# A second-block stage of a two-block transformer kernel: gate evacuations from VectorE to ScalarE, two XC operations from VectorE to GpSimd

## The chip, the cores and the metric

The kernel runs on one core of one Trainium2 chip. The metric is the device time of one execution in microseconds; the numbers given are medians over several runs.

## The reference

Two networks run one after the other on 256 tokens of width 1024. The first has two layers (windowed attention, then bidirectional retention, each with a feed-forward part). The second has two equal layers; each has a feed-forward part, a mixer with three branches (windowed attention, a gated linear recurrence, attention over a memory), and a second feed-forward part. The change is in the recurrence branch of the second network's mixer, and in the head norm of the first network's attention. Cut to that:

```python
proj = h @ w_in[l]                       # q, k, v, xr, yr, cq, gates
xc = causal_conv(xr, conv_w) + conv_b    # width 4, per channel
xb = xc.reshape(B, S, LRU_BLOCKS, LRU_BLOCK)
r  = sigmoid(einsum('bshi,hij->bshj', xb, wa) + ba)
gi = sigmoid(einsum('bshi,hij->bshj', xb, wx) + bx)
log_a = -LRU_C * r * softplus(-lam)
a = exp(log_a)
b = sqrt(1 - exp(2 * log_a)) * gi * xc   # the square root is 1 at token 0
h = scan(a, b)                           # h[t] = a[t] h[t-1] + b[t]
br_lru = (h * gelu(yr)) @ w_lru_out
```

The first network's head norm divides each head of q and k by the root of its mean square.

## The kernel before

Every product goes through one pipeline. A weight matrix is cut into units of 512 rows by 256 columns (four chunks of 128 rows). SyncE loads a unit into one of four slots of `raw`; ScalarE rounds it to `w_hi` (line 1234); VectorE computes `w_lo = raw - w_hi` (line 1776); TensorE then makes three matmuls for each chunk and column half, high by high, high by low, low by high (line 845), 24 matmuls of 256 columns a unit, into an accumulator `acc` of two halves used in turn, one half to a block of 256 output columns. A half is given back by the semaphore `acc_free`, which the engine that empties it raises. TensorE starts a unit when `lo_done` says that its `w_lo` is there, and SyncE reloads a slot of `raw` when the split of that slot is done.

ScalarE and VectorE each work through one fixed order of steps, written out by `head`, `step`, `rest` and `evacuate`. For the job that comes next, `head` splits its first three units and after each of them empties what blocks of the job before have ended; `rest` splits the others, with the evacuations three units behind. An engine with nothing to empty for a job passes `None`.

In the second network's layer the jobs around the change are `yr`, `q`, `kvlru`, `gates`, `cq`, `lru_out` and attention. `kvlru` has four units and six blocks. Units 0 and 1 give k and v (blocks 0 and 1, evacuated to `v_T`, which is the tile `std`, and `k_d`). Units 2 and 3 are the block-diagonal gate weights `wa` and `wx`, split into `w_diag`, and give blocks 2 and 3 (`R`) and 4 and 5 (`GI`), 24 matmuls each (line 1176). Before these, TensorE waits for `xc_ok`, the high and low halves of the convolution's result `XC` in `h_hi` and `h_lo`.

- ScalarE casts `XC` to `h_hi` (line 1705, `xch_ok`) after `head("q")`, then goes on with the split of q's last unit. It also takes a sigmoid over all of `R` and all of `GI` (line 1560) once VectorE has written both blocks of each; these sit in ScalarE's order among the splits of `gates` units 1 and 2 and after unit 2.
- VectorE subtracts for `h_lo` after `head("kvlru")` (line 2373), evacuates all six blocks (lines 2095, 2100, 2105: for `R` and `GI` one addition of the bias to 128x1024), and multiplies `GI` by `XC` (`gated_input`, line 2379) after the first iteration of `gates`. The clamp, the multiply by `XR` and the scan follow, each after another iteration of `gates`.
- GpSimd waits for that product (`gx_ok`), then makes attention's biases `bias2` (line 778), and between them the product with `gy` (line 770) and another subtraction for `h_lo` (line 772).

In the first network, the sums of squares of 20 heads stand in rows 0 to 19 of `sd_b`. The matmul of line 1072 spreads them with `headback` over all 128 rows of both, so VectorE first fills `sd_b` with zeros (line 2165).

Of the kernel before, what the change touches and what calls it, by code (L numbers as in the profile page):

```python
# [23 lines left out]
ALU = mybir.AluOpType  # L24
ACT = mybir.ActivationFunctionType

P = 128
D = 1024
DC = D // P
S = 256  # L30
# [257 lines left out]
GATE_B, CONV_W, FFN1_N, MIX_N, CONV_B, BA, BX, LAM, MEM_N, FFN2_N, CUR = 0, 24, 56, 64, 72, 80, 88, 96, 104, 112, 120  # L288
# [20 lines left out]
def build(nc, a, out, const_at):  # L309
    J = JOBS  # L310
    st = ExitStack()
    with st:
# [3 lines left out]
        def sem(name):  # L316
            return st.enter_context(nc.semaphore(name))
# [11 lines left out]
        h_hi, h_lo = h_all[:, 0], h_all[:, 1]  # L329
        rows = sb("rows", [P, 2 * D])  # L330
        prm = sb("prm", [P, 4, P])
        cur = sb("cur", [P, CUR + 16])
# [31 lines left out]
        def arena(*parts):  # L364
# [38 lines left out]
        v_T = std  # L403
# [5 lines left out]
        acc = st.enter_context(nc.psum_tensor("acc", [P, 2, 2, 512], F32))  # L409
        wk = st.enter_context(nc.psum_tensor("wk", [P, 4, 512], F32))  # L410
# [17 lines left out]
        acc_free = sem("acc_free")  # L428
# [15 lines left out]
        hsq, hss, hstd, hrec, hback, hn, hperm, hrot, hqk, kd_ok = [sem(k) for k in (  # L444
            "hsq", "hss", "hstd", "hrec", "hback", "hn", "hperm", "hrot", "hqk", "kd_ok")]
# [9 lines left out]
        cur_ok, conv_ok, xch_ok, xc_ok, zero_ok = [sem(k) for k in ("cur_ok", "conv_ok", "xch_ok", "xc_ok", "zero_ok")]  # L455
        e2_ok, cl_ok, mu_ok, gx_ok, b_ok, scan_ok, lru_ok, lruh_ok, lru_done = [sem(k) for k in (
            "e2_ok", "cl_ok", "mu_ok", "gx_ok", "b_ok", "scan_ok", "lru_ok", "lruh_ok", "lru_done")]
# [3 lines left out]
        yh_ok, y_ok_c, pooled = sem("yh_ok"), sem("y_ok_c"), sem("pooled")  # L461
        ga_ok, gm_ok = sem("ga_ok"), sem("gm_ok")
        low_ok, half_ok, gz_ok, gu_ok, rg_ok = [sem(k) for k in ("low_ok", "half_ok", "gz_ok", "gu_ok", "rg_ok")]
        sd_zero, ri_ok = sem("sd_zero"), sem("ri_ok")
        fin_t, stored = sem("fin_t"), sem("stored")
        fin_ok = [sem("fin_ok_0"), sem("fin_ok_1")]

# [90 lines left out]
        HEAD_ORDER = [8, 9] + list(range(8))  # L558
# [142 lines left out]
        def _(pool):  # L701
# [59 lines left out]
            for l in range(LAYERS2):  # L761
                pooled_squares("dna", l)

                pool.wait_ge(gx_ok, 1 + l)
                first, _, _ = attn_base("second", l)
                for h in range(WH):
                    if h == 2:

                        pool.wait_ge(scan_ok, 8 + l * 8)
                        pool.tensor_tensor(XC[:], XR[:, :, 0:S], gy[:], ALU.mult).then_inc(lru_ok, 1)  # L770
                        pool.wait_ge(lruh_ok, 1 + l)
                        pool.tensor_tensor(h_lo[:, :, S:2 * S], XC[:], h_hi[:, :, S:2 * S], ALU.subtract).then_inc(lru_done, 1)
                    if h >= 4:

                        pool.wait_ge(m_raw, first + 4 * ((h - 4) // 2) + 4)
                    pool.wait_ge(in_const, 16 * 2)

                    pool.tensor_tensor(bias2[:, h % 4, :], alibi[:, :], slopes[:, h:h + 1].broadcast_to((P, 2 * S)), ALU.mult)\
                        .then_inc(bias_ok, 1)

                for b in range(J["mem_out"].per):
                    pool.wait_ge(mgh_ok, 1 + b + l * 4)
                    pool.tensor_tensor(h_lo[:, 2 * b:2 * b + 2, S:2 * S], gates[:, 2 * b:2 * b + 2, :], h_hi[:, 2 * b:2 * b + 2, S:2 * S],
                                       ALU.subtract).then_inc(mg_done, 1)
                pooled_squares("w_out", l)
                pooled_squares("dnb", l)
# [3 lines left out]
        def _(pe):  # L790
# [277 lines left out]
            for c in range(11):  # L1068
                if c < 10:
                    if c >= 2:  # L1070
                        pe.wait_ge(hn, c - 1)
                    pe.matmul(wk[:, 1 + c % 2, :], headback[:, HEAD_ORDER[c], :], sd_b[:, 0, :], start=True, stop=True).then_inc(hback, 1)
                if c:
                    b = c - 1
                    pe.wait_ge(hn, b + 1)
                    if b >= 2:
                        pe.wait_ge(hrot, b - 1)
                    pe.matmul(part_ps[b % 2][:, 0:S], partner[:, :], qk[:, HEAD_ORDER[b], 0:S], start=True, stop=True).then_inc(hperm, 1)
                beside_first(c - 11)
# [63 lines left out]
            for l in range(LAYERS2):  # L1143
# [14 lines left out]
                for p in range(2):  # L1158
                    unit_ready(job, l, 0, p)
                    for cb in range(2):  # L1160
                        for k in range(KCH):
                            for i, (ws, xs) in enumerate(((w_hi, h_hi), (w_hi, h_lo), (w_lo, h_hi))):
                                mm = pe.matmul(acc[:, 1 - cb, 0, 0:S], ws[:, p, k, cb * P:(cb + 1) * P], xs[:, p * KCH + k, 0:S],
                                               start=(p == 0 and k == 0 and i == 0), stop=(p == 1 and k == KCH - 1 and i == 2))
# [63 lines left out]
        def _(act):  # L1228
# [325 lines left out]
                ins.then_inc(acc_free, 1)  # L1554

            def kvlru(l, it, b):
                if b in (3, 5):
                    dst = R if b == 3 else GI
                    act.wait_ge(acc_free, J["kvlru"].taken(l, 0, b))
                    act.activation(dst[:], dst[:], ACT.Sigmoid).then_inc(ri_ok, 1)  # L1560

            def q_e(l, it, b):
                act.copy(q_2[:, 2 * b:2 * b + 2, :], acc[:, b, :, 0:S]).then_inc(acc_free, 1)
# [31 lines left out]
                    act.wait_ge(hss, c - 1)  # L1595
                act.activation(sq_b[:, c % 2, :], qk[:, c, :], ACT.Square).then_inc(hsq, 1)
            act.wait_ge(hss, 10)
            act.wait_ge(sd_zero, 1)
            act.activation(sd_b[0:20, 0, :], wk[0:20, 0, :], ACT.Sqrt, bias=eps[0:20, 0:1], scale=1.0 / HD).then_inc(hstd, 1)
            act.preload_act_table(ACT.Exp)  # L1600
            for i in range(-SIDE_START - 1, 0):
# [169 lines left out]
        def _(dve):  # L1771
# [34 lines left out]
            def head(name, l=None, prev=None, prev_evac=None):  # L1806

                for p in range(LAG):
                    step(name, l, 0, p)
                    if prev:  # L1810
                        evacuate(prev, prev_evac, prev_layer(prev, name, l), J[prev].iters - 1, J[prev].body + p - LAG)
                if isinstance(prev_evac, tuple):
                    prev_evac[1](prev_layer(prev, name, l), J[prev].iters - 1)

            def rest(name, evac, l=None, between=(), first=LAG):


                job, late = J[name], evac[1] if isinstance(evac, tuple) else None
                for p in range(first, job.body):
                    step(name, l, 0, p)  # L1820
                    evacuate(name, evac, l, 0, p - LAG)

                def one(it):
                    for p in range(job.body):
                        step(name, l, it, p)
                        if p < LAG:
                            evacuate(name, evac, l, it - 1, job.body + p - LAG)
                        else:
                            evacuate(name, evac, l, it, p - LAG)
                        if late and p == LAG:  # L1830
                            late(l, it - 1)

                for n, other in enumerate(between):
                    if n:
                        one(n)
                    other()
                start = max(len(between), 1)
                if job.iters > start:
                    with dve.Fori(start, job.iters) as it:
                        one(it)  # L1840
# [249 lines left out]
                        dve.tensor_tensor(bb(0), bb(0), bb(2), ALU.add).then_inc(mg_ok, 1)  # L2090
                return evac

            def kvlru(l, it, b):
                if b == 0:
                    dve.tensor_copy(v_T[:], acc[:, 0, 0, 0:S]).then_inc(acc_free, 1)
                elif b == 1:

                    for g in range(2):
                        for half in range(2):
                            ins = dve.tensor_copy(k_d[64 * half:64 * half + 64, g, :], acc[64 * g:64 * g + 64, 1, 0, 0:S])  # L2100
                    ins.then_inc(acc_free, 1)
                else:
                    dst, bias = (R, BA) if b < 4 else (GI, BX)
                    c = 4 * (b % 2)
                    dve.tensor_tensor(dst[:, c:c + 4, :], acc[:, b % 2].rearrange("p a (c t) -> p (a c) t", c=2),  # L2105
                                      cur[:, bias + c:bias + c + 4].unsqueeze(2).broadcast_to((P, 4, S)), ALU.add).then_inc(acc_free, 1)

            def modulations(n, layer, src, c0, c1):

                dve.tensor_tensor(mod[:, layer, c0:c1, :], src, prm[:, 0, 48 * layer + c0:48 * layer + c1].unsqueeze(2)  # L2110
# [51 lines left out]
            dve.wait_ge(in_prm, 16 * PRM_DMAS)  # L2162
            dve.wait_ge(soft_ok, 1)
            dve.scalar_tensor_tensor(soft_t[:], soft_in[:], -1.0, soft_in[:], ALU.mult, ALU.min).then_inc(soft_v, 1)
            dve.memset(sd_b[:, 0, :], 0.0).then_inc(sd_zero, 1)
            dve.wait_ge(in_attn, 96)
            dve.wait_ge(hstd, 1)
            dve.reciprocal(sd_b[0:20, 0, :], sd_b[0:20, 0, :]).then_inc(hrec, 1)
# [1 line left out]
            for c in range(11):  # L2170
# [6 lines left out]
                if c:  # L2177
                    b = c - 1
# [139 lines left out]
            for l in range(LAYERS2):  # L2318
# [50 lines left out]
                conv(3)  # L2369
                rest("q", None, l)  # L2370
                head("kvlru", l, "q", None)
                dve.wait_ge(xch_ok, 1 + l)
                dve.tensor_tensor(h_lo[:, :, S:2 * S], XC[:], h_hi[:, :, S:2 * S], ALU.subtract).then_inc(xc_ok, 1)
                rest("kvlru", kvlru, l)
                head("gates", l, "kvlru", kvlru)

                def gated_input():
                    dve.wait_ge(ri_ok, 2 + l * 2)
                    dve.tensor_tensor(GI[:], GI[:], XC[:], ALU.mult).then_inc(gx_ok, 1)

                def clamp():
                    dve.wait_ge(e2_ok, 8 + l * 16)
# [12 lines left out]
                    for c in range(DC):  # L2395
                        dve.tensor_tensor_scan(XR[:, c, 0:S], R[:, c, :], GI[:, c, :], 0.0, ALU.mult, ALU.add).then_inc(scan_ok, 1)

                rest("gates", None, l, [gated_input, clamp, multiply, scan])
                head("cq", l, "gates", None)
                dve.wait_ge(vt_ok, 1 + l)  # L2400
                dve.tensor_copy(v_2[:].rearrange("p r n -> p (r n)"), wk[:, 3, 0:S]).then_inc(v2_ok, 1)
# [66 lines left out]
```

## Time and profile before

| | us |
|---|---|
| median of 3 runs | 2594.54 |
| lowest and highest run | 2586.8, 2594.69 |
| the profiled execution | 2586.8 |
| its span, from the first to the last instruction | 2585.0 |
| TensorE busy (share of the span) | 2485.5 (96%) |
| VectorE busy | 1535.9 (59%) |
| ScalarE busy | 1254.2 (49%) |
| GpSimd busy | 113.3 (4%) |

The profile is of one execution. PE is TensorE, DVE VectorE, ACT ScalarE, POOL GpSimd and SP SyncE. Times in its rows are counted from the start of the span. Layer 0 of the stage in question lies at 1513 to 1550 us, layer 1 at 2176 to 2213.

### The profile page before, as it was taken

The numbers are of one execution on the slowest core, as the hardware profiler recorded it, in microseconds if no ns is written. First come the engines' busy times: TensorE is split into PE (matmuls) and PEld (weight loads), VectorE is DVE, ScalarE is ACT, GpSimd is POOL, SyncE is SP. The second block draws the span as 40 slices with busy tenths as digits, with TensorE's granted clock in tenths as the row PEclk, the third lists the DMA queues.
The fourth block names the chain that finished last, engine by engine and source line by source line (L and its number), as shares of the span: only waits on it lengthen the run. The fifth ranks groups of instructions, "written<-read, shape, count | busy, mean of one in ns | idle before, by whom it ended". The sixth has DMA issues, their size and how long they took to land.

```text
span 2585.0 us, 42115 instructions
## 1 busy us (share of the span) xinstructions
PE 2485.5 (96%) x15422; PEld 2131.8 (82%) x15422; DVE 1535.9 (59%) x2452; ACT 1254.2 (49%) x1911; POOL 113.3 (4%) x104
## 2 busy tenths in 40 slices
PE   7999989999989999999999999999999999999998
PEld 5745678888879976788888989898888899989887
DVE  4166553332264256666776666877667766676874
ACT  3257532222243252554555458655555544865553
POOL 3000000000000000000000001110000000111000
PEclk9999999999999999999999999999999999999999
DMA  8389323333232242465565545356556555444653
GB/s 277 96 269 293 116 74 96 93 96 97 90 114 90 89 136 95 145 194 180 180 186 168 181 146 187 106 173 191 184 180 191 162 174 181 157 133 147 195 181 119
DMA packets 398653, 398.25 MB, mean 154 GB/s; under 512 B 17360, under 2 KB 396768, under 8 KB 398544
## 3 DMA queue, kind: packets, MB, share of 16 engines
q1 hardware_dynamic: 395680, 390.25, 48.3%
q0 software_dynamic: 2864, 6.57, 0.8%
q8 instruction: 66, 1.08, 0.2%
q14 instruction: 43, 0.35, 0.0%
HBM read 395.72 MB, written 1.05 MB: 153 GB/s over the span
## 4 chain that ended last, share of the span: by engine, by line
PE 81%; DVE 6%; issue 5%; ACT 4%; POOL 2%; DMA 1%; SPq 0%; ACTq 0%; DVEq 0%; POOLq 0%
PE acc L845 28%; PE acc L839 25%; PE acc L841 13%; PE acc L824 4%; DVE w_lo L1776 2%; ACT w_hi L1234 2%; PE acc L908 1%; PE wk L975 1%; PE wk L1002 1%; PE acc L1002 1%; PE wk L927 1%; PE acc L1203 1%; PE wk L917 1%; POOL XC L770 1%; PE wk L988 1%
## 5 line engine op out<-in xcount | busy, mean ns | idle before, releaser
L1776 DVE TENSOR_TENSOR w_lo<-raw,w_hi 128x1024 fp32r<-128x1024 f32 (+1 forms) x656 | 803.9, 1239 | 601.4 <-ACT w_hi L1234 600.2
L1234 ACT CAST w_hi<-raw 128x1024 fp32r<-128x1024 f32 (+1 forms) x656 | 669.3, 1032 | 458.1 <-PE acc L845 231.2
L845 PE MATMUL acc<-h_all,w_hi 128*128 128x256 f32 (+1 forms) x3360 | 750.6, 319 | 22.6 <-DVE GI L2105 6.9
L839 PE MATMUL acc<-h_all,w_hi 128*128 128x512 f32 x2016 | 710.5, 397 | 4.5 <-DVE h_all L1885 4.5
L845 PEld LDWEIGHTS acc<-h_all,w_hi 128*128 128x128 f32 x3360 | 563.3, 193 | 67.5 <-issue 20.8
L841 PE MATMUL acc<-h_all,w_lo 128*128 128x256 f32 x2016 | 565.5, 281 | 0.0
L845 PE MATMUL acc<-h_all,w_lo 128*128 128x256 f32 (+1 forms) x1680 | 534.9, 318 | 0.0
L839 PEld LDWEIGHTS acc<-h_all,w_hi 128*128 128x128 f32 x2016 | 379.7, 188 | 94.3 <-issue 4.7
L841 PEld LDWEIGHTS acc<-h_all,w_lo 128*128 128x128 f32 x2016 | 382.2, 190 | 0.2
L845 PEld LDWEIGHTS acc<-h_all,w_lo 128*128 128x128 f32 x1680 | 323.8, 193 | 20.7
L839 PE MATMUL acc<-hid_all,w_hi 128*128 128x512 f32 x880 | 312.4, 398 | 2.9 <-DVE w_lo L1776 2.9
L841 PE MATMUL acc<-hid_all,w_lo 128*128 128x256 f32 x880 | 247.6, 281 | 0.0
L839 PEld LDWEIGHTS acc<-hid_all,w_hi 128*128 128x128 f32 x880 | 165.2, 188 | 45.4 <-DVE w_lo L1776 4.8
L841 PEld LDWEIGHTS acc<-hid_all,w_lo 128*128 128x128 f32 x880 | 165.9, 189 | 0.1
L824 PE MATMUL acc<-w_hi,h_all 128*128 128x256 f32 x704 | 128.1, 284 | 0.0
L2027 DVE TENSOR_TENSOR act_buf<-acc,act_buf 128x512 f32<-128x512 f32 x110 | 76.0, 691 | 84.0 <-ACT act_buf L1500 54.4
L824 PEld LDWEIGHTS acc<-w_hi,h_all 128*128 128x128 f32 x704 | 110.1, 192 | 1.8 <-issue 1.7
L845 PE MATMUL acc<-hid_all,w_hi 128*128 128x512 f32 x352 | 111.0, 396 | 0.0
L824 PE MATMUL acc<-w_lo,h_all 128*128 128x256 f32 x352 | 99.6, 283 | 0.0
L845 PEld LDWEIGHTS acc<-hid_all,w_hi 128*128 128x128 f32 x352 | 66.1, 188 | 15.9
L1500 ACT COPY act_buf<-acc 128x512 f32<-128x512 f32 x55 | 32.3, 587 | 94.4 <-PE acc L841 94.4
L1397 ACT ACTIVATE probs<-probs,soft_nm 128x256 f32<-128x256 f32 (+1 forms) x112 | 63.2, 564 | 26.9 <-DVE soft_nm L1925 26.1
(346 smaller groups left out, 2446.8 us busy)
## 6 DMA issues: line engine op xcount, KB each, us to landing
raw<-in_w_in_dram SPq DMA_DIRECT2D x100, 512.0 KB, 3.9
ring<-in_ada_w_dram SPq DMA_DIRECT2D x88, 512.0 KB, 5.6
raw<-in_ffn_w_in_dram SPq DMA_DIRECT2D x88, 512.0 KB, 3.6
raw<-in_ffn_w_gate_dram SPq DMA_DIRECT2D x88, 512.0 KB, 3.9
raw<-in_ffn_w_up_dram SPq DMA_DIRECT2D x88, 512.0 KB, 3.9
raw<-in_ffn_w_down_dram SPq DMA_DIRECT2D x80, 512.0 KB, 4.3
raw<-in_ret_w_qkvg_dram SPq DMA_DIRECT2D x48, 512.0 KB, 3.7
raw<-in_ffn_w_out_dram SPq DMA_DIRECT2D x40, 512.0 KB, 3.5
```

Of the source, the lines that this page charges most:

```text
L770: pool.tensor_tensor(XC[:], XR[:, :, 0:S], gy[:], ALU.mult).then_inc(lru_ok, 1)
L824: mm = pe.matmul(o, xs[:, kk, x], ws[:, s, k, :], start=(u == 0 and k == 0 and i == 0 and not (packed and n % 2)), stop=(last and k == nk ...
L839: pe.matmul(o, w_hi[:, s, k, c], merged[:, :, kk, t], start=(u == 0 and k == 0), stop=False, skip_group_check=True)
L841: mm = pe.matmul(o[:, S:2 * S], w_lo[:, s, k, c], merged[:, 0, kk, t], start=False, stop=(last and k == nk - 1), skip_group_check=True)
L845: mm = pe.matmul(o, ws[:, s, k, c], xs[:, kk, t], start=(u == 0 and k == 0 and i == 0), stop=(last and k == nk - 1 and i == 2))
L908: mm = pe.matmul(acc[32 * k:32 * k + 32, b % 2, 0, 0:S], c_wide[:, u * KCH + k, :], landed[:, k, :], start=(u == 0), stop=(u == 1), tile_p ...
L1002: mm = pe.matmul(G["out"], G["v"][c], G["probs_t"][:, 2 * (q % 2) + n, c, :], start=(c == 0), stop=(c == tiles - 1), skip_group_check=True)
L1234: act.copy(w_hi[:, s, 0:nk, :], raw[:, s, 0:nk, :]).then_inc(hi_done, 1)
L1397: act.activation(pr, pr, ACT.Exp, bias=snm[:, i % 8:i % 8 + 1], accum_out=ssum[:, i % 8:i % 8 + 1])\
L1500: act.copy(up, acc[:, 1, :, S:2 * S]).then_inc(low_ok, 1)
L1776: dve.tensor_tensor(w_lo[:, s, 0:nk, :], raw[:, s, 0:nk, :], w_hi[:, s, 0:nk, :], ALU.subtract).then_inc(lo_done, 1)
L2027: dve.tensor_tensor(part, acc[:, b, :, 0:S], part, ALU.add).then_inc(acc_free, 1)
```

## The change

Five things are edited.

1. ScalarE empties all six blocks of `kvlru`: two of them with plain copies, the four gate blocks with sigmoids of 128x256 straight out of the accumulator, the bias in the same instruction, four a block. The two sigmoids of 128x2048 and the semaphore `ri_ok` go, and VectorE's `kvlru` evacuation goes.
2. The subtraction for `h_lo` of `XC` is done by GpSimd, when `xch_ok` is there.
3. The product of `GI` and `XC` is done by GpSimd, when `acc_free` says that the last block of `kvlru` is out, and ahead of the biases.
4. In VectorE's order `gated_input` becomes an empty entry.
5. The matmul of line 1072 reads 20 rows of `headback` and `sd_b`; the memset and its semaphore `sd_zero` go.

```diff
@@ GpSimd
-                pool.wait_ge(gx_ok, 1 + l)
+                pool.wait_ge(xch_ok, 1 + l)
+                pool.tensor_tensor(h_lo[:, :, S:2 * S], XC[:], h_hi[:, :, S:2 * S], ALU.subtract).then_inc(xc_ok, 1)
+
+                pool.wait_ge(acc_free, J["kvlru"].done(l))
+                pool.tensor_tensor(GI[:], GI[:], XC[:], ALU.mult).then_inc(gx_ok, 1)
@@ TensorE
-                    pe.matmul(wk[:, 1 + c % 2, :], headback[:, HEAD_ORDER[c], :], sd_b[:, 0, :], start=True, stop=True).then_inc(hback, 1)
+                    pe.matmul(wk[:, 1 + c % 2, :], headback[0:20, HEAD_ORDER[c], :], sd_b[0:20, 0, :], start=True, stop=True).then_inc(hback, 1)
@@ ScalarE
             def kvlru(l, it, b):
-                if b in (3, 5):
-                    dst = R if b == 3 else GI
-                    act.wait_ge(acc_free, J["kvlru"].taken(l, 0, b))
-                    act.activation(dst[:], dst[:], ACT.Sigmoid).then_inc(ri_ok, 1)
+                if b == 0:
+                    act.copy(v_T[:], acc[:, 0, 0, 0:S]).then_inc(acc_free, 1)
+                elif b == 1:
+
+                    for g in range(2):
+                        for half in range(2):
+                            ins = act.copy(k_d[64 * half:64 * half + 64, g, :], acc[64 * g:64 * g + 64, 1, 0, 0:S])
+                    ins.then_inc(acc_free, 1)
+                else:
+                    dst, bias = (R, BA) if b < 4 else (GI, BX)
+                    for c in range(4):
+                        cc = 4 * (b % 2) + c
+                        ins = act.activation(dst[:, cc, :], acc[:, b % 2, c // 2, (c % 2) * S:(c % 2) * S + S], ACT.Sigmoid,
+                                             bias=cur[:, bias + cc:bias + cc + 1])
+                    ins.then_inc(acc_free, 1)
...
-            act.wait_ge(sd_zero, 1)
@@ VectorE
-            def kvlru(l, it, b):
-                if b == 0:
-                    dve.tensor_copy(v_T[:], acc[:, 0, 0, 0:S]).then_inc(acc_free, 1)
-                elif b == 1:
...
-            dve.memset(sd_b[:, 0, :], 0.0).then_inc(sd_zero, 1)
...
-                dve.wait_ge(xch_ok, 1 + l)
-                dve.tensor_tensor(h_lo[:, :, S:2 * S], XC[:], h_hi[:, :, S:2 * S], ALU.subtract).then_inc(xc_ok, 1)
-                rest("kvlru", kvlru, l)
-                head("gates", l, "kvlru", kvlru)
-
-                def gated_input():
-                    dve.wait_ge(ri_ok, 2 + l * 2)
-                    dve.tensor_tensor(GI[:], GI[:], XC[:], ALU.mult).then_inc(gx_ok, 1)
+                rest("kvlru", None, l)
+                head("gates", l, "kvlru", None)
...
-                rest("gates", None, l, [gated_input, clamp, multiply, scan])
+                rest("gates", None, l, [lambda: None, clamp, multiply, scan])
```

## Rows read from the trace of the kernel before

**Rows 1.** The page's chain that ended last, shares by engine.

```profile
PE 81%; DVE 6%; issue 5%; ACT 4%; POOL 2%; DMA 1%; SPq 0%; ACTq 0%; DVEq 0%; POOLq 0%
```

**Rows 2.** TensorE's waits, 1513 to 1550 us: total, times, longest.

```profile
PE acc L845 <- DVE GI L2105: 3.4, 1, 3.4
PE acc L1176 <- DVE R L2105: 1.4, 1, 1.4
PE acc L1163 <- ACT rows L1563: 0.7, 1, 0.7
PE acc L1176 <- DVE std L2095: 0.6, 1, 0.6
```

**Rows 3.** Timeline of ScalarE in the stage: start, duration, instruction, idle before.

```profile
1513.52 1.90 ACT L1705 CAST h_all<-XC 128x2048 fp32r<-128x2048 f32 x1 [0.78 <-DVE XC L2360]
1515.32 1.99 ACT L1234 CAST w_hi<-raw 128x1024 fp32r<-128x1024 f32 x2
...
1535.35 1.92 ACT L1560 ACTIVATE R<-R 128x2048 f32<-128x2048 f32 x1 [5.17 <-DVE R L2105]
1537.18 1.02 ACT L1234 CAST w_hi<-raw 128x1024 fp32r<-128x1024 f32 x1
...
1543.76 1.28 ACT L1281 ACT_TABLE_LOAD   x1
```

**Rows 4.** Timeline of VectorE in the stage.

```profile
1516.40 3.62 DVE L1776 TENSOR_TENSOR w_lo<-raw,w_hi 128x1024 fp32r<-128x1024 f32 x3 [2.91 <-ACT w_hi L1234]
...
1529.06 0.42 DVE L2095 COPY std<-acc 128x256 f32<-128x256 f32 x1 [0.52 <-PE acc L1163]
...
1532.88 2.36 DVE L2105 TENSOR_TENSOR R<-acc,cur 128x1024 f32<-128x1024 f32 x2 [0.51 <-PE acc L1176]
...
1539.37 2.35 DVE L2105 TENSOR_TENSOR GI<-acc,cur 128x1024 f32<-128x1024 f32 x2
```

**Rows 5.** Timeline of TensorE in the stage.

```profile
1522.04 0.28 PE L845 MATMUL acc<-h_all,w_lo 128*128 128x256 f32 x1
...
1534.25 3.04 PE L1176 MATMUL acc<-h_all,w_diag 128*128 128x256 f32 x24 [1.41 <-DVE R L2105]
1540.72 0.75 PE L845 MATMUL acc<-h_all,w_hi 128*128 128x256 f32 x2 [3.43 <-DVE GI L2105]
...
1544.05 0.47 PE L845 MATMUL acc<-h_all,w_hi 128*128 128x256 f32 x2
```

**Rows 6.** Stretches: width, busy time of PE, PEld, DVE, ACT, POOL, granted clock, DMA.

```profile
1540.70:1544.40 3.70, 3.68 (x18) 3.68 (x19) 1.02 (x1) 2.54 (x2) 0.00 (x0) 0.54 0.46 140
1550.00:1560.00 10.00, 10.00 (x84) 9.85 (x83) 5.95 (x5) 9.94 (x16) 1.68 (x2) 1.00 0.47 134
```

**Rows 7.** GpSimd on tile XC: ns min/median/max, first and last start.

```profile
L770 POOL TENSOR_TENSOR XC<-XR,gy x2: 7783/7785/7787, 1586.1 to 2248.6; 128x2048 f32<-128x2048 f32 x2
...
L772 POOL TENSOR_TENSOR h_all<-XC,h_all x2: 4634/4634/4634, 1614.5 to 2277.1; 128x2048 fp32r<-128x2048 f32 x2
```

**Rows 8.** VectorE's line 1776, 1590 to 1597 us and 1612 to 1626 us.

```profile
L1776 DVE TENSOR_TENSOR w_lo<-raw,w_hi x2: 1211/2704/4197, 1590.7 to 1594.8; 128x1024 fp32r<-128x1024 f32 x2
...
L1776 DVE TENSOR_TENSOR w_lo<-raw,w_hi x4: 1212/2055/4814, 1615.4 to 1624.1; 128x1024 fp32r<-128x1024 f32 x4
```

**Rows 9.** ScalarE's line 1553 (gates evacuations): durations, and two of them in the timeline.

```profile
L1553 ACT ACTIVATE gates<-acc,cur x48: 465/474/486, 1553.0 to 2274.8; 128x256 f32<-128x256 f32 x24, 128x256 f32 x24
...
1552.98 0.84 ACT L1553 ACTIVATE gates<-acc,cur 128x256 f32<-128x256 f32 x2
```

**Rows 10.** TensorE at 97.42 us in the timeline, and the stretch after it.

```profile
97.42 0.70 PE L845 MATMUL acc<-h_all,w_hi 128*128 128x512 f32 x2 [1.83 <-DVE w_lo L1776]
...
97.40:102.00 4.60, 4.58 (x20) 3.81 (x21) 4.03 (x6) 2.25 (x3) 0.00 (x0) 1.00 0.75 226
```

**Rows 11.** The page's loads of the input projection: KB each, us to landing.

```profile
raw<-in_w_in_dram SPq DMA_DIRECT2D x100, 512.0 KB, 3.9
```

**Rows 12.** TensorE's first head-norm matmuls in the timeline.

```profile
134.08 3.40 PE L1072 MATMUL wk<-sd_b,headback 128*128 128x512 f32 x4 [4.21 <-DVE sd_b L2168]
```

More of the change, by code:

```diff
@@ L463, in build @@
         low_ok, half_ok, gz_ok, gu_ok, rg_ok = [sem(k) for k in ("low_ok", "half_ok", "gz_ok", "gu_ok", "rg_ok")]
-        sd_zero, ri_ok = sem("sd_zero"), sem("ri_ok")
         fin_t, stored = sem("fin_t"), sem("stored")
@@ L2091, in branch @@
                 return evac
-            def kvlru(l, it, b):
-                if b == 0:
-                    dve.tensor_copy(v_T[:], acc[:, 0, 0, 0:S]).then_inc(acc_free, 1)
-                elif b == 1:
[L2098 to L2106, printed above, removed]
             def modulations(n, layer, src, c0, c1):
```

## The prediction

> **What bounds the kernel now.** I read the page's chain first: TensorE holds most of it [rows 1], so one microsecond taken from or given to TensorE is one microsecond of the span, and work on the other engines counts only where TensorE waits for it. Then, for the stretch of the change (kvlru, once in each layer of the second block), TensorE's waits: four of them, 3.4, 1.4, 0.7 and 0.6 us [rows 2]. Layer 1 repeats layer 0 662.6 us later (2277.1 - 1614.5 [rows 7]), so I work in layer 0 and double. The 0.7 us wait is for a q copy that the change leaves alone; the other three, 5.4 us a layer, are for the evacuations that it moves. The timelines of ScalarE and VectorE say why the longest is so long. The last gate matmuls start at 1534.25 and end 3.04 us later, at 1537.29 [rows 5], but VectorE takes the accumulator only at 1539.37 [rows 4]. In its queue stands the split of gates unit 2, which waits for ScalarE's cast at 1537.18, and that cast stands behind the sigmoid of R at 1535.35, which waited for VectorE's own evacuation of R [rows 3, 4]. TensorE starts again at 1540.72, and at half clock: granted 0.54 over the next 3.7 us, with 18 matmuls [rows 6]. The pace at full clock is (3.04 - 0.28) / 23 = 0.12 us a matmul [rows 5]; at the low level (1.2 GHz instead of 2.4) it is 3.33 / 16 = 0.21. The sixteen slow matmuls from 1540.72 to 1544.05 [rows 5] cost 3.33 - 16 x 0.12 = 1.4 us more. So at most 5.4 + 1.4 = 6.8 us a layer are to be had, 13.6 in all, 0.5% of the span.
>
> **The parts of the change.** The sum is made against the profiled execution, 2586.8 us (span 2585.0). It is the lowest of the three runs; the median is 2594.54, 7.7 us above it, and I carry the difference over to the median.
>
> (1) The subtraction for the low half of XC goes from VectorE to GpSimd and starts as soon as ScalarE's cast is done: 1513.52 + 1.90 = 1515.42 [rows 3], with GpSimd idle. The same form, fp32r out of two 128x2048 inputs in SBUF, took 4.63 us on GpSimd [rows 7]. It would run from 1515.46 to 1520.09. Its consumers, the gate matmuls, start behind the v_T copy of 1529.06 [rows 4], so as a result it is early by 9 us. But look at what VectorE's splits did while GpSimd ran such an operation [rows 7, 8]. A split takes 1.21 us. The one begun at 1590.7, under the multiply that ended at 1586.1 + 7.8 = 1593.9, took 4.20 and ended 1.0 us after it. The first of four begun from 1615.4 on, under the subtraction that ended at 1614.5 + 4.6 = 1619.1, is the longest, 4.81, and ended 1.1 us after it. A two-input fp32 operation of VectorE stands still until GpSimd's is over. In the new place the split of q's last unit stands there: its w_hi is cast just behind XC's cast, and it ran from 1516.40 [rows 3, 4]. Now it ends at 1520.09 + 1.09 = 1521.18. TensorE wants it at the start of that unit's 24 matmuls: 1522.04 - 23 x 0.12 = 1519.28 [rows 5]. New wait: **+1.9 us**. The kvlru splits behind it (1.2 us each) are ready before TensorE gets to them, and the loads that wait for these splits to free their slots, 3.9 us to landing [rows 11], are wanted some 6 us later.
>
> The Trainium skill says the same of the pair (SBUF - State Buffer, section SBUF: two separate sides): the SBUF ports that VectorE and GpSimd share are an exclusive lock, held for a whole instruction, and the loser blocks. By that rule the trace agrees [rows 8], and the rule speaks against the change. The Trainium skill's page GPSIMD Engine Reference (section Elementwise - side-by-side cycle accounting) puts this size at 4497 ns where the row has 4634; by the page the new wait would be 1.8 instead of 1.9 us.
>
> (2) Blocks 0 and 1 (v_T and k_d) are copied by ScalarE at the same trigger. A 128x256 ScalarE operation out of PSUM takes 0.47 us [rows 9], VectorE's copy 0.42 [rows 4]; TensorE's wait is the 0.6 us before the gate matmuls [rows 2]. Between 0 and 0.1 either way: **0**. The cast of gates unit 1, now behind these five copies, is wanted 10 us later.
>
> (3) Blocks 2 and 3 (R): VectorE took one 128x1024 operation a block, 2.36 for two [rows 4]. ScalarE takes four sigmoids a block, at a pace of 0.84 - 0.47 = 0.37, the first block after 3 x 0.37 + 0.47 = 1.58 us; 0.84 is what two of this kind take in the gates stretch, and 0.47 is one [rows 9]. TensorE's wait was 1.41 with about 1.2 of evacuation in it [rows 2, 5], and becomes 1.41 + 0.36: **+0.35 us**. The second half's accumulator is free at 8 x 0.37, as the twelve matmuls before it end. From below this could be 0.2 (four at 0.31 after a shorter first), from above 0.6.
>
> (4) Blocks 4 and 5 (GI): nothing stands before them on ScalarE now but one cast of 1.02 us [rows 3], which is over while the matmuls run (3.04). The wait becomes 1.58 + 0.15 = 1.73 us where it was 3.43 [rows 5]: **-1.7 us**. The big sigmoids (1.92 for R [rows 3], and one like it for GI) vanish: ScalarE's next work, the table load at 1543.76, starts when block 5 is done, which is 1537.29 + 1.9 + 0.35 + 3.08 = 1542.6, 1.1 us earlier. That matters, for ScalarE is busy 9.94 of 10 us in the gates stretch [rows 6], so it has little room there; but its start moves up by more than TensorE's, and it does not hold TensorE back through this change.
>
> (5) The clock. TensorE starts gates at 1540.72 + 1.9 + 0.35 - 1.7 = 1541.3, after a pause of 1.7. A pause of 1.83 us left the granted clock at 1.00 [rows 10]; the fall came after 3.43 [rows 5, 6]. So I take it that the slow matmuls go: **-1.4 us**.
>
> (6) GI times XC goes to GpSimd: 1542.6 to 1547.3 at 4.63. VectorE's split of gates unit 3 is cast at about 1545 and ends at 1548.4; TensorE wants it at 1541.3 + 3 x 2.88 = 1549.9. The product is wanted by VectorE's multiply two iterations of gates later, the two biases behind it only by attention. **0**. What VectorE loses in work nobody waits for beyond what is counted above.
>
> (7) The head sums: one memset of VectorE, issued long before ScalarE writes over it, and a contraction over 20 rows instead of 128, in 20 matmul instructions paced by their 512 columns; TensorE's 4.2 us wait, up to 134.08, is for a reciprocal that stays [rows 12]. **0**, within half a microsecond.
>
> Sum for a layer: 1.9 + 0.35 - 1.7 - 1.4 = -0.85 us, two layers **-1.7 us**: 2585.1 for the profiled execution, 2592.8 for the median.
>
> **The rivals.** Within 0.3% (7.8 us) is about what a measurement of this kernel cannot tell from no change.
> (a) The forecast: the new wait for GpSimd eats what the shorter evacuation gives; only the clock is won. 0.6.
> (b) The clock falls all the same, since the stretch now holds pauses of 1.9, 0.6, 1.8 and 1.7 us. Then +0.55 a layer, 2595.6. Against it only the single pause of [rows 10]. 0.13.
> (c) GpSimd's subtraction does not stand in the split's way, as that is finished by both in turns. Then no 1.9: -2.75 a layer, -5.5, 2589.0. Against it both rows of [rows 8]. 0.09.
> (d) The other side: GpSimd takes for such an operation what the multiply of 128x2048 took, 7.79 [rows 7]. I think that part of those was its own waiting for a VectorE operation that was already running, but it may be the price of the operation. Then the split ends 3.15 us later, the pause becomes 5.1 and the clock falls (+1.4), and the product in (6) ends so late that gates unit 3 is 1.6 us late: -0.85 + 3.15 + 1.4 + 1.6 = +5.3 a layer, +10.6, 2605.1. It makes the kernel slower by over 0.3% from about 7.1 us an operation. 0.06.
> (e) The move of the evacuations does nothing, since ScalarE comes to block 4 no earlier than VectorE did (a late load holds the cast of gates unit 2). Then 1.7 + 1.4 of the gain goes, -0.85 becomes +2.25 a layer, +4.5, 2599.0. Against it: loads land in 3.9 us [rows 11], and the slot is free as soon as VectorE has split the gate weights, some 10 us before the cast. 0.06.
> Something elsewhere that I don't see: 0.06, half to each side.
>
> **The numbers.** Predicted is (a), 2592.8. The runs of one kernel spread by 7.9 us here, more than any of (a) to (c) moves it, so the range reaches from 2584 (the profiled execution's level less the forecast) to 2600, with (b), (c) and (e) in it; outside stand (d) and most of the unseen. Faster by over 0.3%: 0.07, from the unseen (0.03) and from a (c) that comes with shorter evacuations, or falls on the low side of the spread (0.04). Slower by over 0.3%: 0.09, (d) with 0.06 and the unseen with 0.03. Same: 0.84.
>
> **What would show it.** After the change, the split of q's last unit should last over 4 us, and TensorE should have a wait for it of 1.9 us near 1521; the wait at the first R evacuation should be 1.7 to 1.8 and that before gates 1.7, with the clock at 1.00 behind it. GpSimd's subtraction should take 4.6 and its product 4.6. The prediction is wrong if the product or the split holds TensorE a second time, if the clock falls, or if q's last split is not stretched.

## The result and the profile after

The kernel got slower. After the change the median is 2606.32 us (5 runs, 2603.89 to 2608.22), before it 2592.01 us (5 runs beside them, 2586.8 to 2594.69): a ratio of 1.0055, 95% interval 1.004 to 1.0069. The forecast was 2592.8, added up from the three-run median of 2594.54, with a range up to 2600. The profiled execution of the changed kernel took 2607.67 us, with a span of 2605.9.

Most of the difference lies in one slice of the page. These are its rows of TensorE's granted clock in 40 slices of 65 us, of the kernel before and then of the kernel after:

```profile
PEclk9999999999999999999999999999999999999999
```

```profile
PEclk9979999999999999999999999999999999999999
```

The third slice, 130 to 195 us, holds the head norm of the first network, the place of the change's fifth edit. Its loop reaches from the first matmul that spreads the head sums to the first attention score. First the stretches of the kernel before: width, busy time of PE, PEld, DVE, ACT, POOL with instruction counts, granted clock, DMA share, GB/s; the first row is the whole loop, the others its beginning.

```profile
134.08:156.30 22.22, 21.32 (x113) 9.01 (x113) 18.22 (x40) 6.32 (x12) 0.00 (x0) 0.92 0.60 188
134.00:139.00 5.00, 4.92 (x9) 2.37 (x10) 2.24 (x5) 0.00 (x0) 0.00 (x0) 0.66 0.25 79
139.00:144.00 5.00, 5.00 (x36) 2.16 (x35) 4.91 (x12) 2.02 (x4) 0.00 (x0) 1.00 0.26 78
```

The same of the kernel after:

```profile
135.27:172.86 37.59, 37.28 (x113) 11.41 (x113) 19.24 (x40) 6.31 (x12) 0.00 (x0) 0.55 0.38 117
135.00:140.00 5.00, 4.73 (x6) 1.65 (x6) 1.71 (x3) 0.00 (x0) 0.00 (x0) 0.50 0.30 95
140.00:145.00 5.00, 5.00 (x7) 1.50 (x6) 3.12 (x7) 0.00 (x0) 0.00 (x0) 0.50 0.00 0
150.00:155.00 5.00, 5.00 (x23) 1.46 (x22) 3.32 (x8) 2.37 (x5) 0.00 (x0) 0.69 0.80 252
155.00:160.00 5.00, 5.00 (x14) 1.38 (x14) 2.00 (x5) 1.68 (x3) 0.00 (x0) 0.50 0.47 142
175.00:180.00 5.00, 4.60 (x52) 1.90 (x45) 4.04 (x21) 4.13 (x14) 0.00 (x0) 1.00 0.95 302
```

The same 113 matmuls take 37.59 us instead of 22.22, which is 15.4 us more, and TensorE is busy for 37.28 of them: it waits for nobody. Busy time times clock is nearly the same, 21.32 x 0.92 = 19.6 before and 37.28 x 0.55 = 20.5 after. So TensorE does the same work at a lower clock: 0.50 is the 1.2 GHz level, 1.00 the 2.4 GHz level. Before, the clock falls to the low level in the loop's first microsecond, behind a pause of 4.2 us [rows 12], and is at 1.00 again from 138 us on. After, it comes up near 149 us, falls again at 152 us with no gap in TensorE's work, and is back at 1.00 for good only when the attention that follows is running. By the distances between starts, the twenty edited matmuls take 7.2 us of the 15.4 more, the 93 others 8.2.

Single calls in the timeline of the kernel after show both levels:

```profile
135.27 3.77 PE L1075 MATMUL wk<-sd_b,headback 20*128 20x512 f32 x4 [4.21 <-DVE sd_b L2165]
...
150.64 1.12 PE L1075 MATMUL wk<-sd_b,headback 20*128 20x512 f32 x2
...
157.82 2.07 PE L1075 MATMUL wk<-sd_b,headback 20*128 20x512 f32 x2
```

and one of the kernel before, at 1.00:

```profile
143.85 1.13 PE L1072 MATMUL wk<-sd_b,headback 128*128 128x512 f32 x2
```

At equal clock a call over 20 rows takes what one over 128 rows takes, 1.12 and 1.13 us (x2: each call is recorded as two matmuls). The pause ahead of the first call is as before, 4.21 us.

The stage that the prediction worked on came out as forecast in this execution. TensorE's waits there after the change, 1536 to 1570 us (total, times, longest), answer to [rows 2]:

```profile
PE acc L848 <- DVE w_lo L1789: 1.8, 1, 1.8
PE acc L1179 <- ACT R L1572: 1.8, 1, 1.8
PE acc L848 <- ACT GI L1572: 1.7, 1, 1.7
PE acc L1166 <- ACT rows L1577: 0.7, 1, 0.7
PE acc L1179 <- ACT std L1561: 0.6, 1, 0.6
```

VectorE's three splits beside the new place of the subtraction, with the group of that line in 1536 to 1545 us (min/median/max ns) behind them, and GpSimd's two new operations (the last two rows):

```profile
1537.17 7.06 DVE L1789 TENSOR_TENSOR w_lo<-raw,w_hi 128x1024 fp32r<-128x1024 f32 x3 [2.91 <-ACT w_hi L1237]
```

```profile
L1789 DVE TENSOR_TENSOR w_lo<-raw,w_hi x3: 1211/1212/4794, 1537.2 to 1543.0; 128x1024 fp32r<-128x1024 f32 x3
```

```profile
L764 POOL TENSOR_TENSOR h_all<-XC,h_all x2: 4610/4613/4616, 1536.3 to 2197.9; 128x2048 fp32r<-128x2048 f32 x2
L767 POOL TENSOR_TENSOR GI<-GI,XC x2: 4627/4627/4627, 1563.4 to 2225.0; 128x2048 f32<-128x2048 f32 x2
```

The first split begins 0.9 us after GpSimd's subtraction and takes 4.79 us where 1.21 is its length; it ends at 1537.17 + 4.79 = 1541.96, and TensorE, which has waited 1.8 us for it, starts at 1542.02. The matmuls that start gates, and the stretch behind them, answer to [rows 5, 6]:

```profile
1561.97 0.50 PE L848 MATMUL acc<-h_all,w_hi 128*128 128x256 f32 x2 [1.74 <-ACT GI L1572]
```

```profile
1561.90:1565.60 3.70, 3.63 (x30) 3.64 (x31) 0.00 (x0) 3.67 (x6) 2.22 (x1) 1.00 0.47 142
```

The clock is 1.00 there, where it was 0.54. From the start of ScalarE's cast of XC to the same matmul at the end of gates' second unit, layer 0 takes 1567.70 - 1534.29 = 33.41 us, where it took 1547.95 - 1513.52 = 34.43: 1.0 us less, and 0.9 less in layer 1.

So 15.4 us more in the head norm and 1.9 less in the two layers make 13.5, where the medians differ by 14.3. The two profiled executions differ by more, 2607.67 - 2586.8 = 20.9 us. The remaining 7.4 us lie in stretches in which the kernels are the same: 1.2 us ahead of the loop, 4.2 between the loop and the first cast of XC, the rest behind it. Read in steps of 4 us, TensorE's clock stands at the low level for about 44 us of the 1361 between loop and cast in the changed kernel's trace, for about 34 of 1357 before. Work takes twice as long there, so by an estimate from these numbers the 10 us account for up to 5. Low stretches of this kind also stand in the trace of the kernel before, one of them with TensorE busy all the time:

```profile
172.00:175.00 3.00, 3.00 (x16) 1.49 (x14) 0.00 (x0) 0.69 (x3) 0.00 (x0) 0.51 1.10 350
```

Why one execution has more of them than another is not explained here.

### The profile page after: what moved, and what is told of

The parts are those of the page before. It is cut to its first block, busy times and chain, and to the rows that moved or that the text cites. A ratio compares the mean times of both kernels' runs of the same rounds, so it can differ in the third digit from the quotient of the medians.

```text
span 2605.9 us, 42125 instructions
## 1 busy us (share of the span) xinstructions
PE 2504.9 (96%) x15422; PEld 2133.5 (82%) x15422; DVE 1525.9 (59%) x2429; ACT 1262.1 (48%) x1949; POOL 133.7 (5%) x108
## 3 DMA queue, kind: packets, MB, share of 16 engines
HBM read 395.72 MB, written 1.05 MB: 152 GB/s over the span
## 4 chain that ended last, share of the span: by engine, by line
PE 81%; DVE 7%; ACT 5%; issue 5%; POOL 2%; DMA 1%; SPq 0%; ACTq 0%; DVEq 0%; POOLq 0%
PE acc L848 27%; PE acc L842 25%; PE acc L844 12%; PE acc L827 4%; DVE w_lo L1789 2%; ACT w_hi L1237 2%; PE acc L911 1%; PE wk L978 1%; PE wk L1005 1%; PE acc L1005 1%; PE wk L1075 1%; PE wk L930 1%; PE acc L1206 1%; PE wk L920 1%; POOL XC L773 1%
## 5 line engine op out<-in xcount | busy, mean ns | idle before, releaser
L1789 DVE TENSOR_TENSOR w_lo<-raw,w_hi 128x1024 fp32r<-128x1024 f32 (+1 forms) x656 | 815.3, 1257 | 614.0 <-ACT w_hi L1237 612.8
```

The costliest lines, as they stand in the source:

```text
L1789: dve.tensor_tensor(w_lo[:, s, 0:nk, :], raw[:, s, 0:nk, :], w_hi[:, s, 0:nk, :], ALU.subtract).then_inc(lo_done, 1)
```

## The experiments

Each kernel below was run beside the kernel before on the same chip, and its ratio is against those runs. The theories are named in the expectations themselves.

### The head norm alone, undone and done

Undone: the changed kernel with 128 rows and the zeros back (in the diffs of this section `...` stands for the rest of a line, and the waits for `sd_zero` are not shown).

```diff
+            dve.memset(sd_b[:, 0, :], 0.0).then_inc(sd_zero, 1)
-                    pe.matmul(wk[:, 1 + c % 2, :], headback[0:20, HEAD_ORDER[c], :], sd_b[0:20, 0, :], ...)
+                    pe.matmul(wk[:, 1 + c % 2, :], headback[:, HEAD_ORDER[c], :], sd_b[:, 0, :], ...)
```

> The changed kernel with the matmul of line 1072 back at 128 rows, and the memset with it. Theory H: the 20-row contraction costs the 15.4 us by which the changed trace is longer between its first matmul of that line and the third block of attention scores (135.27 to 177.91 against 134.08 to 161.35), as TensorE's granted clock stands at 0.50 to 0.69 there. Then this kernel takes the time before less the 2 us of the kvlru stage, 2590 (ratio 0.998 to 1.000). Rival L: the loss lies in the rest of the program (the two traces drift apart by another 7.5 us there). Then this kernel stays some 5 to 7 us slower than before, ratio 1.002 to 1.003.

Done alone: the kernel before with 20 rows and without the memset, and nothing else of the change.

> The kernel before with the 20-row matmul alone, memset gone. Theory H: plus 15 us, ratio 1.006, the clock at 0.5 to 0.7 in the head norm. Rival L: within 0.3% of before. Rival M, that the loss comes from both parts together: less than half of it here.

Undone, the time is 2588.91 us (12 runs), a ratio of 0.9987, interval 0.9978 to 0.9997. Alone, it is 2604.89 us (6 runs), 1.005, interval 1.0034 to 1.0067. Theory H came out, L and M are out. The loop in each, as a stretch; undone first:

```profile
135.57:157.83 22.26, 21.31 (x113) 8.92 (x113) 18.18 (x40) 6.32 (x12) 0.00 (x0) 0.93 0.59 188
```

```profile
132.95:170.53 37.58, 37.22 (x113) 11.41 (x113) 19.24 (x40) 6.32 (x12) 0.00 (x0) 0.55 0.38 118
```

The loop is 22.3 us at 0.93 with 128 rows and 37.6 us at 0.55 with 20, whatever is done in the second network. The fifth edit is the whole loss: alone it costs 0.50%, and without it the change is worth -0.13%, where the prediction had -1.7 us, 0.07%.

The profile of the undone kernel shows something else in the second network. Its stage is the changed kernel's, with the same five waits. But here the granted clock falls within a microsecond behind the new wait for q's last split, in both layers. First that wait, then the stretches behind it in layer 0 and layer 1:

```profile
1523.51 0.50 PE L849 MATMUL acc<-h_all,w_hi 128*128 128x256 f32 x2 [1.84 <-DVE w_lo L1791]
...
1523.50:1527.70 4.20, 4.19 (x23) 4.19 (x24) 3.51 (x4) 0.00 (x0) 0.00 (x0) 0.61 0.65 174
2185.90:2190.10 4.20, 4.15 (x22) 4.15 (x23) 3.55 (x4) 0.00 (x0) 0.00 (x0) 0.59 0.64 163
```

From the cast of XC to the end of gates' second unit each layer takes 34.9 us here, half a microsecond more than before and 1.5 more than in the changed kernel's trace.

### 64 rows

This parts the row count from the memset, which stays: `headback[0:64, ...]`, `sd_b[0:64, ...]` in the kernel before.

> The kernel before with 64 rows in the matmul of line 1072 instead of 128, the memset kept. If what counts is how much of the array works, the clock in the head norm lies between the 128-row trace (0.91 from 134 to 152) and the 20-row one (0.55), or at one of the two levels; the time is 0 to 15 us above before. If the 20-row loss came from the form of the instruction (a row count below 32), this one takes the time before.

It took 2601.02 us (4 runs), a ratio of 1.0037, interval 1.0022 to 1.0051.

```profile
135.99:175.98 39.99, 39.69 (x112) 11.88 (x112) 19.31 (x40) 6.33 (x12) 0.00 (x0) 0.51 0.35 110
```

With the memset in place and 44 rows of zeros in the contraction the clock still stays low. So it is not the missing memset, nor the time at which `sd_b` is there, and half of the rows are not enough. The median lies 9.9 us above that of the kernel before (0.37% by the ratio), and the profile's loop alone is 17.8 us longer. The timed runs of these few-row kernels spread widely (2598.64 to 2610.26 here, 2593.58 to 2608.74 for 20 rows alone). Their mean granted clocks go with the times: for 20 rows alone 0.984 in the run of 2593.58 us and 0.979 in the two of 2605.12 and 2608.74. I take it that the stretch at the low level is not equally long in each execution; that it is the loop's stretch is not shown, with one loop in view for each kernel.

This trace also has the kernel before's wait of 3.4 us ahead of gates, and in layer 0 the clock does not fall behind it:

```profile
1561.53 0.50 PE L845 MATMUL acc<-h_all,w_hi 128*128 128x256 f32 x2 [3.44 <-DVE GI L2105]
...
1561.50:1565.20 3.70, 3.67 (x30) 3.68 (x31) 1.03 (x1) 2.54 (x2) 0.00 (x0) 1.00 0.48 140
```

So the length of a pause does not by itself say whether the clock falls: 1.84 us were enough above, and 3.44 were not here.

Nor does a contraction over 64 rows lower it wherever it stands. The attention behind the loop has such matmuls in every kernel. In the kernel before they run at 1.00, between others over 128 rows:

```profile
156.30 1.13 PE L975 MATMUL wk<-k_dup,qk 64*128 64x512 f32 x4 [0.90 <-DVE qk L2184]
...
156.30:161.35 5.05, 4.65 (x49) 1.70 (x49) 2.93 (x12) 2.52 (x8) 0.00 (x0) 1.00 0.87 277
```

### 96 rows

The same with `0:96`.

> The kernel before with a contraction over 96 rows (76 of them zeros) instead of 128 in the twenty head-norm matmuls, the memset kept; nothing else. With 128 rows the loop takes 22.2 us at a granted clock of 0.92, with 64 rows 40.0 us at 0.51. Theory G (the more of the array's rows are in use, the more clock is granted, by degrees): the loop lies between, 25 to 35 us, clock 0.6 to 0.85, and the time is 3 to 13 us above the kernel before. Rival T (anything short of 128 rows counts alike, or 96 is already enough): the loop is at one of the two ends, 38 to 40 us or 22 us. I take G, without much ground.

It took 2591.49 us (10 runs), a ratio of 0.9994, interval 0.9984 to 1.0003: no difference.

```profile
135.55:157.70 22.15, 21.25 (x112) 9.13 (x113) 18.32 (x40) 6.32 (x12) 0.00 (x0) 0.92 0.59 185
```

I had expected a clock between the ends, and that fell. With 96 rows the loop is that of 128 rows, with 64 that of 20. In this loop nothing came out between the two.

### Was the loop low because of the pause ahead of it?

Behind the 4.2 us pause the clock is low at the start of the loop with few rows and with many, so the few rows might only keep it from coming back. Four products of 128 rows and 512 columns were put into the pause, into a bank that the loop overwrites, so that it starts at the high level.

```diff
+            pe.wait_ge(hsq, 10)
+            for _ in range(4):
+                pe.matmul(wk[:, 1, :], headback[:, 0, :], sq_b[:, 0, :], start=True, stop=True)
             pe.wait_ge(hrec, 1)
```

Once with 20 rows, in the kernel before with the fifth edit alone:

> The same four matmuls in the pause, in the kernel before with the 20-row matmul. If the 20-row loop is slow because it never recovers from the pause, the fill gives the 15 us back: 22 us or less for the loop. If the loop itself lowers the clock, it starts at 1.00 and falls within a few matmuls: 33 to 36 us for the loop instead of 37.6, ratio 1.004 to 1.005.

and once with 128 rows, in the version of the change that keeps the head norm and VectorE's subtraction (below):

> The kernel with the head norm undone and the subtraction on VectorE, and four more matmuls of 128 rows and 512 columns in TensorE's pause before the head norm's loop (their result is overwritten unread). Theory P: the pause of 4.2 us lowers the clock (0.66 at the loop's start before); filled, the clock stays at 1.00 and the loop takes 20 us instead of 22.2: 2 us less than without them. Rival: the clock falls all the same, or the loop is bound by VectorE: level or slower.

With 20 rows the time is 2604.58 us (4 runs), a ratio of 1.0053, interval 1.0034 to 1.0072. The filled pause, the start of the loop at 133.20, and the whole loop:

```profile
129.00:134.00 5.00, 4.42 (x10) 1.83 (x11) 3.34 (x1) 1.96 (x2) 0.00 (x0) 1.00 1.08 356
134.00:139.00 5.00, 5.00 (x10) 1.76 (x9) 3.73 (x8) 0.00 (x0) 0.00 (x0) 0.73 0.04 13
139.00:144.00 5.00, 5.00 (x21) 1.58 (x21) 2.74 (x7) 0.33 (x2) 0.00 (x0) 0.50 0.03 3
...
133.20:171.07 37.87, 37.45 (x113) 11.27 (x113) 19.25 (x40) 6.31 (x12) 0.00 (x0) 0.55 0.37 115
```

The loop begins at 1.00 and the clock falls inside it, while TensorE is busy 5.00 of every 5.00 us. The theory of a loop that only fails to recover is out. The forecast of 33 to 36 us missed low: at 37.87 us, filling the pause gave the loop nothing back.

With 128 rows the same filling removes the low stretch at the start; the first row is the filled pause and the loop's first microsecond, the second the whole loop:

```profile
134.00:139.00 5.00, 4.42 (x11) 1.82 (x10) 3.39 (x2) 1.58 (x2) 0.00 (x0) 1.00 1.01 333
137.79:158.56 20.77, 19.87 (x112) 8.29 (x112) 18.19 (x40) 6.32 (x12) 0.00 (x0) 1.00 0.65 199
```

20.77 us instead of 22.2 is 1.4 us less. The time is 2585.32 us (7 runs), 0.9971, interval 0.996 to 0.9983; beside the same version without the filling (0.9978) that can't be told apart.

### Full-row work among the few-row calls

The last question is whether the presence of few-row calls or the lack of full ones keeps the clock down. Each call of the loop got an extra product over 128 rows ahead of it, into the bank that it then overwrites.

```diff
+                    pe.matmul(wk[:, 1 + c % 2, :], headback[:, HEAD_ORDER[c], :], sq_b[:, 0, :], start=True, stop=True)
                     pe.matmul(wk[:, 1 + c % 2, :], headback[0:20, HEAD_ORDER[c], :], sd_b[0:20, 0, :], ...)
```

> The kernel before with 20 rows and no memset, and ahead of each of the ten loop calls of the head norm one extra product of headback with the squares over all 128 rows and 512 columns, into the same bank, overwritten unread (so the output is the reference's). Theory F (the granted clock follows how much of the array the stream of matmuls uses, and the extra work lifts that): though the loop has ten more calls, it gets shorter than the 37.6 us of 20 rows alone, some 26 to 33 us at a clock of 0.85 to 1.00, and the time is 4 to 11 us above the kernel before. Rival A (any 20-row matmul in the stream keeps the clock at its low level): the clock stays near 0.55 and the loop takes 47 to 55 us, so 25 to 33 us above the kernel before.

It took 2606.85 us (5 runs), a ratio of 1.0051, interval 1.0035 to 1.0068. The whole loop and its two parts:

```profile
135.43:176.03 40.60, 39.85 (x132) 12.76 (x133) 18.65 (x40) 6.32 (x12) 0.00 (x0) 0.80 0.33 104
135.43:151.00 15.57, 15.57 (x18) 4.82 (x18) 4.62 (x9) 0.00 (x0) 0.00 (x0) 0.50 0.07 25
152.00:176.00 24.00, 23.29 (x114) 7.44 (x112) 14.04 (x31) 6.32 (x12) 0.00 (x0) 1.00 0.51 160
```

Both theories missed with a number. The loop, 40.6 us, is neither the 26 to 33 of the one nor the 47 to 55 of the other. But the clock tells them apart: from 152 us on it stands at 1.00 for 24 us in which the 20-row calls go on, and in no trace of 20-row calls alone did it stay there that long. One such call from each part:

```profile
137.41 2.07 PE L1074 MATMUL wk<-sd_b,headback 20*128 20x512 f32 x2
...
155.24 1.12 PE L1074 MATMUL wk<-sd_b,headback 20*128 20x512 f32 x2
```

So a few-row call in the stream does not by itself hold the clock down. With full-row work beside it the clock stayed up once it was up; that this work brings the clock up is not shown, for in the first 15.6 us the same pairs of calls ran at 0.50 throughout. The length missed for two reasons. The clock was low for some 16 us at the start, where it is for 3.5 us with 128 rows alone. And the ten extra calls took 14 us, four at nearly 2 us each and six at 1.05. As a cure it is worthless; rows of zeros cost nothing.

### The second network's edits, one at a time

The subtraction alone: the kernel before, with GpSimd's new subtraction and without VectorE's.

> The kernel before with the subtraction for h_lo on GpSimd alone. By term (1) TensorE waits 1.8 us for q's last split in each layer, all else shifted by it: +3.6 us, ratio 1.001 to 1.002. Rival: the wait is made good later in the stage, and the time is that of before.

The time is 2595.2 us (11 runs), 1.0013, interval 1.0004 to 1.0022. Its two longest waits of TensorE in the stage, and VectorE's splits:

```profile
PE acc L848 <- DVE GI L2108: 3.4, 1, 3.4
PE acc L848 <- DVE w_lo L1779: 1.8, 1, 1.8
```

```profile
1518.07 7.06 DVE L1779 TENSOR_TENSOR w_lo<-raw,w_hi 128x1024 fp32r<-128x1024 f32 x3 [2.92 <-ACT w_hi L1237]
```

Layer 1 took 1.5 us more than layer 0 up to the start of gates, as the clock fell behind the wait for `w_lo` there too.

The other way round: the changed kernel with the head norm undone and the subtraction back on VectorE.

> Head norm undone as in the first, and the subtraction for h_lo back on VectorE; evacuations on ScalarE and the GI product on GpSimd stay. By term (1) of the prediction TensorE's wait of 1.8 us for q's last split goes in both layers: 3.6 us less than the kernel with the head norm undone, 5.5 less than before, ratio to before 0.998. Rival: the wait comes back at another place and the two are level.

The time is 2584.81 us (11 runs), 0.9978, interval 0.9968 to 0.9988. The wait for `w_lo` is gone, and the others stay:

```profile
PE acc L1177 <- ACT R L1570: 1.8, 1, 1.8
PE acc L846 <- ACT GI L1570: 1.7, 1, 1.7
```

And the evacuations alone on ScalarE, with both operations on XC left on VectorE (the product then waits for the last evacuation instead of for `ri_ok`).

> The kernel before with the evacuations of kvlru on ScalarE alone; both XC operations stay on VectorE, the head norm as before. By terms (3) to (5) of the prediction: -2.75 us a layer, 5.5 in all, ratio 0.998, level with the kernel that has the product on GpSimd too (term (6) is 0). Rival: the product on VectorE holds a split back, and this one is 1 us or more slower than that.

The time is 2584.61 us (10 runs), 0.9975, interval 0.9965 to 0.9984. The subtraction on GpSimd is thus a loss of at least 1.8 us a layer and 0.13% in all, the evacuations a gain of 0.25%, and the product on GpSimd changes nothing that these runs show (0.9978 with it, 0.9975 without). In the traces of these last two versions the stage takes 31.35 us in either layer, 3.0 less than before, with the clock at 1.00. They and the version with the filled pause are faster than both kernels of the case; between themselves the runs don't tell them apart.

## Why the prediction was wrong

The step that failed is **(7)**: "a contraction over 20 rows instead of 128, in 20 matmul instructions paced by their 512 columns", priced at "0, within half a microsecond". It measured +15.4 us in the profile, and +0.50% (about 13 us) in the timed runs of that edit alone. The premise holds at equal clock (1.12 against 1.13 us a call), but I took the clock to be given. With 20 rows TensorE's granted clock stays at or falls to the low level for most of the loop, though TensorE is busy nearly without a gap, and the other 93 matmuls pay for it (8.2 us) as well as the twenty that were edited (7.2). The range and the chances missed for the same reason: the clock stood in the prediction only as something that pauses decide, in (5) and rival (b), and the 0.06 for the unseen was all that the head norm had.

The Trainium skill (TensorE: Matmul & The Clock Gate, section Why this matters for your kernels) says that a single matmul with a contraction of 32 takes as long as one of 128. By that sentence the edit costs nothing, as I had it, and the trace agrees with it call by call at equal clock; for the loop it is off by 15.4 us. The same section asks for no long gaps between matmuls to keep the clock up. Here the clock fell with no gap, and in the undone kernel behind one of 1.84 us; the measurement decides.

Of the other steps all but (5) held in every trace that has them:

- **(1)** VectorE's split stretched: 4.79 us, and a wait of 1.81 where +1.9 was forecast. Rival (c), that the split is not in the way, is out, and so is (d): GpSimd took 4.61 us, not 7.8.
- **(2)** 0: the wait before the gate matmuls is 0.6 as before.
- **(3)** +0.35: the wait for R went from 1.41 to 1.75 us (forecast 1.76).
- **(4)** -1.7: the wait for GI went from 3.43 to 1.74 (forecast 1.73). Rival (e) is out.
- **(5)** -1.4: in the changed kernel's trace the clock is 1.00 behind that wait, through pauses of 1.8, 1.8 and 1.7 us in one stretch. In the trace of the undone kernel, with the same waits, it fell behind the first of them in both layers, and the stage took 0.5 to 0.6 us more than before, where rival (b) had +0.55. So (b) is not out: it came in one trace of two. The step took the pause's length to decide [rows 10], and the runs do not bear that out.
- **(6)** 0: GpSimd's product took 4.63 us; the split of gates unit 3 stood still under it (3.39 us instead of 1.21), and TensorE did not wait for it.

By the waits this is 1.81 + 0.34 - 1.69 - 1.4 = -0.94 a layer where the clock stays up, by the stage's length in the changed kernel's trace -1.0, and the forecast was -0.85. By itself the second network's part moves the median from 2591.1 to 2588.9 (the head norm undone), by 2.2 us (0.03 to 0.22%) where -1.7 was forecast. The waits there were right in each part; that the sum fits so well is in part luck, since the clock's term came in one trace and not in the other.

Three things stay open. Why 96 rows act like 128 and 64 like 20 in this loop, when 64 rows in the attention behind it do not, isn't known; no kernel was run with other counts, or with few rows put into another loop. Why the clock falls behind the same wait in one execution and not in another isn't known either. And the 7.4 us by which the two profiled executions differ beyond the known places go for the most part with longer low stretches of the clock, whose cause was not found.

## What to carry to other kernels

In this loop unused contraction rows were free in time only as long as the clock stayed up. In a dense stream, leave the contraction full, with zeros in the unused rows, rather than cut it (here the zeros cost nothing that the runs show); before cutting one, look at the granted clock of its stretch and at what the other matmuls there would pay at half of it.

An elementwise operation moved from VectorE to GpSimd can cost more than it saves if a two-input operation of VectorE that TensorE wants stands beside it: look up what VectorE runs in the new place, not how long it is idle in total.

When a change has several edits, the smallest one deserves its own line of doubt. Here the one that got a single sentence cost four times what the others gave together (0.50% against 0.13%).

One profiled execution does not settle what the clock does behind a short pause. Before a saving is booked on it, look at the same stretch in the traces of several kernels that share it.

## What the runs showed of the hardware that was not expected

TensorE's granted clock went from 1.00 to 0.50 in a loop in which TensorE was busy all the time, when ten of its calls used 20 of 128 rows; in the same loop it was 0.51 on average with 64 rows, 0.92 with 96 and 0.92 with 128. Rows filled with zeros count as rows here: in the kernel before, 108 of the 128 are zeros. With one full-row call beside each few-row call the clock came back to 1.00 in the middle of the loop and stayed there to its end.

The clock fell behind a wait of 1.84 us in one trace and stayed at 1.00 behind one of 3.44 us in another, where 3.43 us had brought it down in the kernel before.
